# Expert stage of a two-layer block: one 128-column token tile, unsplit down weights, and a new order of work within an expert

## The reference, cut to what matters

```python
combine = jnp.sum(one_hot(expert_id, 32) * weight[..., None], axis=1)      # two experts for each token
hid = silu(einsum('td,edf->tef', tk, w1)) * einsum('td,edf->tef', tk, w3)  # 1024 -> 256, twice
hid = hid * c[:, :, None]
y   = einsum('tef,efd->td', hid, w2)                                       # 256 -> 1024
```

## Time and profile before

| what | value |
|---|---|
| median of 3 runs | 1771.48 us (1768.0 to 1773.71) |
| the profiled execution | 1772.76 us |
| its span, first to last instruction | 1770.7 us |
| TensorE busy | 1523.5 us, 86% |
| VectorE busy | 948.3 us, 54% |
| ScalarE busy | 714.9 us, 40% |
| mean granted TensorE clock | 0.925 of full speed |

### The profile page before, as it was taken

One profiled execution on the slowest core, in us unless ns is written; L12 is line 12 of the kernel. 1 busy time (PEld: TensorE's weight loads), 2 busy tenths in 40 slices (PEclk: granted clock), 3 DMA queues, 4 the chain that ended last, 5 costly groups with the idle time before them and its releaser, 6 DMA issues.

```text
span 1770.7 us, 17596 instructions
## 1 busy us (share of the span) xinstructions
PE 1523.5 (86%) x7159; PEld 1147.0 (65%) x7159; DVE 948.3 (54%) x1301; ACT 714.9 (40%) x1043; POOL 68.2 (4%) x80
## 2 busy tenths in 40 slices
PE   5999997798786963899999991989697899999999
PEld 4888775586565842555555551868585877678887
DVE  3444246623763445788888874675545535321334
ACT  4333334424443220666666662244322215652231
POOL 1000000000000000111011101000000000000000
PEclk9999998998997986899999996999897988999999
DMA  6422221122104430999999984220101003002241
GB/s 197 168 96 75 96 73 66 68 75 72 70 26 161 152 119 23 307 327 340 331 336 335 329 294 156 72 71 26 47 1 48 1 24 119 1 1 72 95 143 48
DMA packets 80348, 224.01 MB, mean 127 GB/s; under 512 B 9044, under 2 KB 10182, under 8 KB 76167
## 3 DMA queue, kind: packets, MB, share of 16 engines
q1 hardware_dynamic: 71558, 193.73, 32.3%
q0 software_dynamic: 6144, 20.71, 3.5%
q10 hardware_dynamic: 2560, 8.39, 1.3%
HBM read 200.00 MB, written 22.81 MB: 126 GB/s over the span
## 4 chain that ended last, share of the span: by engine, by line
PE 59%; DVE 25%; ACT 11%; DMA 2%; issue 2%; SPq 1%; POOL 0%; DVEq 0%; POOLq 0%; ACTq 0%
PE PS L502 14%; PE PS L504 14%; PE PS L503 14%; DVE wlo L1152 7%; DVE htlo L1152 5%; PE PS L928 4%; ACT whi L1950 3%; PE PS L499 3%; DVE ylo L1152 2%; ACT work L1950 2%; PE PS L1077 2%; ACT yhi L1950 2%; PE PS L1068 1%; ACT hthi L1950 1%; DVE work L1561 1%
## 5 line engine op out<-in xcount | busy, mean ns | idle before, releaser
L1152 DVE TENSOR_TENSOR wlo<-raw,whi 128x2048 fp32r<-128x2048 f32 x74 | 169.1, 2291 | 356.3 <-ACT whi L1950 356.3
L1950 ACT ACTIVATE whi<-raw 128x2048 fp32r<-128x2048 f32 x74 | 141.2, 1912 | 334.9 <-PE PS L504 333.5
L499 PE MATMUL PS<-consts,work 128*128 128x128 f32 (+1 forms) x652 | 100.7, 298 | 125.9 <-DVE work L1178 53.2
L502 PE MATMUL PS<-whi,hthi 128*128 128x512 f32 x480 | 200.1, 417 | 9.2 <-ACT work L1950 6.4
L502 PE MATMUL PS<-hthi,whi 128*128 128x512 f32 x480 | 198.3, 413 | 5.1 <-ACT scratch L1950 2.8
L503 PE MATMUL PS<-wlo,hthi 128*128 128x512 f32 x480 | 190.9, 398 | 0.0
L504 PE MATMUL PS<-whi,htlo 128*128 128x512 f32 x480 | 190.8, 398 | 0.0
L504 PE MATMUL PS<-hthi,wlo 128*128 128x512 f32 x480 | 190.0, 396 | 0.0
L503 PE MATMUL PS<-htlo,whi 128*128 128x512 f32 x480 | 189.5, 395 | 0.0
L499 PEld LDWEIGHTS PS<-consts,work 128*128 128x128 f32 (+1 forms) x652 | 85.2, 182 | 155.1 <-DVE work L1178 54.4
L1950 ACT ACTIVATE work<-PS 128x512 f32<-128x512 f32 (+3 forms) x204 | 103.3, 531 | 88.6 <-PE PS L992 51.2
(11 more groups left out here) (320 smaller groups left out, 2600.3 us busy)
## 6 DMA issues: line engine op xcount, KB each, us to landing
raw<-in_w_in SPq DMA_DIRECT2D x44, 1024.0 KB
raw<-in_w SPq DMA_DIRECT2D x80, 512.0 KB
scratch<-in_w SPq DMA_DIRECT2D x48, 512.0 KB
raw<-in_w SPq DMA_DIRECT2D x19, 1024.0 KB
scratch<-in_w SPq DMA_DIRECT2D x13, 1024.0 KB
raw<-in_w_gate SPq DMA_DIRECT2D x8, 1024.0 KB
raw<-in_w_out SPq DMA_DIRECT2D x8, 1024.0 KB
y_scratch<-work ACTq DMA_DIRECT2D x32, 256.0 KB, 7.1
```

The source lines that it names most:

```text
L499: return e.transpose(o, i, ident[0:n, 0:n])
L502: e.matmul(o, lh, rh, start=start, stop=False)
L1152: tt(lo, raw_place(j), as_f32(hi), SUB).then_inc(*ve.mark("lo", j))
L1950: return e.activation(o, i, f, bias=bias, scale=scale)
```

## The change

1. `bring` puts the high and the low part of a token tile side by side in one tile `G` of 128 columns. `up` multiplies that tile by the high and by the low half of the weights: 16 matmuls in place of 24. Partitions 0 to 63 of the result are the products of the high tokens, 64 to 127 those of the low tokens. ScalarE copies the lower half down (`low_half`) and VectorE adds (`join`) into `UPS`.
2. The down unit is not split. `down` multiplies the hidden tile, unsplit and padded with zeros to 128 columns (`HT`), by the raw unit in plain fp32: 4 matmuls in place of 12. A down unit now keeps its raw slot until `down` is done (`pe["unit", ...]`).
3. Slots in the stage: 7 raw (3 of `raw`, 2 in the second halves of `yhi`/`ylo`, 2 lent by `scratch`), 4 split. Two more units can be loaded and two more up units are split before the stage.
4. Order in step n: TensorE up(n), hand_over(n-1), bring(n+1), down(n-1). ScalarE split, hand_over(n-1), low_half(n), split, bring(n+1), gate_hidden(n), down(n-1). VectorE split, bring(n+1), join(n), low_tokens(n+1), hidden(n), split. The splits of step n are those of up(n+2).

```diff
-    LENT_RAW, LENT_SPLIT = 2, 3
+    LENT_RAW, LENT_SPLIT = 4, 2
...
+    G = yhi[:, 0:4, :].rearrange("p a n -> p (a n)").rearrange("p (u k n) -> p u k n", u=2, k=KD)
+    GHI, GLO = G[:, :, :, 0:CAP], G[:, :, :, CAP:2 * CAP]
+    HT = y_plain[:, 1, 0, :].rearrange("p (u k n) -> p u k n", u=2, k=2)
...
-                    m = passes(ps[0:CAP, :], GHI[:, u, kk, :], GLO[:, u, kk, :], wh[:, :, k, :], wl[:, :, k, :],
-                               kk == 0, kk == KD - 1)
+                    e.matmul(ps, G[:, u, kk, :], wh[:, :, k, :], start=kk == 0, stop=False)
+                    m = e.matmul(ps, G[:, u, kk, :], wl[:, :, k, :], start=False, stop=kk == KD - 1)
...
+                on.wait_ge(*raw_got[raw_slot[j]][j])
+                on.wait_ge(*ve["blank"])
+                on.wait_ge(*ac["out", "hidden", n])
                 for k in range(2):
-                    m = passes(PS[0:CAP, bank.of[key], :], HHI[:, u, k, :], HLO[:, u, k, :], wh[:, k, cols],
-                               wl[:, k, cols], k == 0, k == 1)
+                    m = e.matmul(ps, HT[:, u, k, :], w[:, k, cols], start=k == 0, stop=k == 1)
...
         for n in range(NE + 1):
+            if n < NE:
+                up(n)
+            if n:
+                hand_over(n - 1)
             if n + 1 < NE:
                 bring(n + 1)
-            if n:
-                hand_over(n - 1)
-            if n < NE:
-                up(n)
             if n:
                 down(n - 1)
...
+            elif raw_prior[j] in whole:
+                on.wait_ge(*pe["unit", raw_prior[j]])
             elif raw_prior[j] is not None:
                 on.wait_ge(*ve["lo", raw_prior[j]])
...
+        def join(n):
+            u = n % 2
+            on.wait_ge(*ac["low half", n])
+            tt(UPS[:, u, :], UPS[:, u, :], inside("up", n)[0:CAP, :], ADD).then_inc(*ve.mark("out", "up", n))
...
         for n in range(NE + 1):
+            if n + 2 < NE:
+                split()
+            if n:
+                hand_over(n - 1)
+            if n < NE:
+                low_half(n)
+            if n + 2 < NE:
+                split()
             if n + 1 < NE:
                 bring(n + 1)
```

More of the change, by code:

```diff
@@ L346, in build @@
     UNITS = len(units)
+    whole = {unit["down", n][0] for n in range(NE)}
+    to_split = [j for j in range(UNITS) if j not in whole]
     raw_slot, split_slot, raw_prior, split_prior = {}, {}, {}, {}
     raw_in, split_in = {}, {}
+    for q, j in enumerate(to_split):
+        q -= to_split.index(MOE) if j < TWO else to_split.index(TWO) - 1
+        split_slot[j] = q % NS if j < MOE or j >= TWO else q % (NS + LENT_SPLIT)
+        split_prior[j] = split_in.get(split_slot[j])
+        split_in[split_slot[j]] = j
     for j in range(UNITS):
@@ L783, in hand_over @@
             pv = ps[:, 0:2 * CAP].rearrange("p (k n) -> p k n", k=2)
-            on.wait_ge(*ve["out", "up", n])
+            on.wait_ge(*ve["hidden", n])
             for k in range(2):
@@ L807, in down @@
             u, j = n % 2, unit["down", n][0]
-            wh, wl = (a.rearrange("p (k n) -> p k n", k=2) for a in split_place(j))
+            w = raw_place(j).rearrange("p (k n) -> p k n", k=2)
             for half in range(2):
[L810 to L815, removed]
+                cols = slice(half * BANK, half * BANK + BANK)
+                ps = fresh("down", n, half)
+                on.wait_ge(*raw_got[raw_slot[j]][j])
+                on.wait_ge(*ve["blank"])
+                on.wait_ge(*ac["out", "hidden", n])
                 for k in range(2):
-                    m = passes(PS[0:CAP, bank.of[key], :], HHI[:, u, k, :], HLO[:, u, k, :], wh[:, k, cols],
-                               wl[:, k, cols], k == 0, k == 1)
-                m.then_inc(*pe.mark(*key))
-                bank.filled(key)
+                    m = e.matmul(ps, HT[:, u, k, :], w[:, k, cols], start=k == 0, stop=k == 1)
+                m.then_inc(*pe.mark("down", n, half))
+                bank.filled(("down", n, half))
             pe.also("unit", j)
@@ L1146, in split @@
         def split():
-            j = next_unit[0]
+            j = to_split[next_unit[0]]
             next_unit[0] += 1
@@ L2173, in scalar @@
             split()
-        normalise("n2", g2, lambda i: ve["out", "wo", 1, i])
+        normalise("n2", g2, lambda i: ve["out", "wo", 1, i], [split, split])
         on.wait_ge(*ve["ex"])
@@ L2212, in scalar @@
         bring(0)
-        for _ in range(LENT_SPLIT):
-            split()
         for n in range(NE + 1):
+            if n + 2 < NE:
+                split()
+            if n:
+                hand_over(n - 1)
+            if n < NE:
+                low_half(n)
+            if n + 2 < NE:
+                split()
             if n + 1 < NE:
                 bring(n + 1)
[L2218 to L2221, removed]
             if n < NE:
-                if next_unit[0] < TWO:
-                    split()
                 gate_hidden(n)
-                if next_unit[0] < TWO:
-                    split()
             if n:
                 down(n - 1)
+        split()
         ac.also("experts")
@@ L2584, in sync @@
         e.dma_start(xw, xv).then_inc(*xw_got.mark("all"))
-        for j in range(first_out + NR, MOE + NS + NR):
+        for j in range(first_out + NR, MOE + NS + NR + 2):
             load(j)
@@ L2590, in sync @@
         e.dma_start(xn_dram.rearrange("(i p) d -> p i d", p=P), xs).then_inc(*xn_put.mark("all"))
-        for j in range(MOE + NS + NR, TWO + NR + 1):
+        for j in range(MOE + NS + NR + 2, TWO + NR + 1):
             load(j)
```

80 lines of the change are left out of this document (42 added, 38 removed).

## The result

The changed kernel takes **1883.36 us** (median of 4 runs, 1880.01 to 1886.51) against 1770.28 us (1768.0 to 1773.71, 4 runs) for the kernel before: a ratio of 1.0631, 95% interval 1.0611 to 1.065. The forecast of 1820 us had the direction and the mechanism; the time lies 33 us above its range.

What follows compares the result with a forecast made beforehand. The prediction took a VectorE and ScalarE loop of 10.99 us an expert to bound the kernel before, DMA 0.3 us behind; 26 x (13.1 - 10.99) = 55, less 6, gives +49 on 1772.8: forecast 1820 us, range 1777 to 1850.

Steps and rivals of the forecast that it cites:

- the mechanism: Expert stage: down done, load of up(n+3) issued, unit landed, ScalarE's split, hand-over, next down; one new loop per expert.
- The work per engine: Expert stage, busy time per expert: VectorE about 7.5 us, ScalarE about 7.3, TensorE 8.9, against 10.99 us an expert before.
- the prediction's own sign of being wrong: Wrong if down's matmuls differ much from 0.95 us, scalings are 10.7 us apart with DMA at its limit, or ScalarE never idles.
- the sum of the loop's length: Expert stage: 5.1 + 0.8 + 1.9 + 0.3 + 3.8 + 0.2 = 12.1 us an expert, 13.1 with the clock's fall.
- down's end to the unit usable: Loop's load: 5.1 us, from a lone load's 4.6 plus wake, issue and notice, and 0.8 for the store sharing the engines.
- The clock: TensorE in the stage: granted clock about 0.8, its fall meeting down and adding 1.0 us an expert, bounds 0 and 2.
- The first four experts: Start of the stage: DMA engines get four units, then run dry; 42 us expected where it was 40.
- The tail: Stage's end after the last scaling: no splits or subtraction in the last two steps, so 26 us shrinks by some 9.
- The loop at full clock: Rival for the expert stage: the loop without the clock's fall, +23 us, 1795 us; chance 0.25.
- The longer loop: Rival for the expert stage: transfers slowed by 1.4 us or down wholly at 1.2 GHz, 14.5 us an expert, 1857 us; chance 0.12.
- The rival by which DMA sets the pace: Rival for the expert stage: the loop doesn't bind, DMA does at 10.7 us an expert, about -21, 1751 us; chance 0.12.
- The lone load of the prediction: A 1.05 MB load in the kernel before, issued at 590.41 with nothing beside it, taking 4.6 us to its last byte.

Runs made afterwards that it cites:

- edit 1: Changed kernel with the seven raw slots dealt out as four for up units and three for down units: 1740.99 us, 0.9787 of the kernel before.
- edit 2: Changed kernel with one raw slot fewer, six in place of seven: 1945.07 us, 1.0953 of the kernel before.
- edit 4: Changed kernel with four unneeded fp32 matmuls added before down's wait, to keep TensorE busy: 1844.84 us, 1.0389 of the kernel before.
- edit 5: Changed kernel with two of the four fp32 matmuls of down left out: 1800.68 us, 1.0128 of the kernel before.
- edit 6: Changed kernel storing 4 of each expert's 64 rows, the rest zeroed once near the start: 1876.07 us, 1.0565 of the kernel before.
- edit 7: Changed kernel with SyncE waiting for the unit held by down to land before issuing the next two: 1845.77 us, 1.0395 of the kernel before.
- edit 3: Changed kernel with ScalarE's hand-over put ahead of the first split in each step: 1811.4 us, 1.0207 of the kernel before.

## Why the prediction was right and wrong

**The mechanism was right.** The wait, the unit behind it, the split in front of the hand-over and the burst of three are in the chain as they were derived from the order of the code. That the loop goes through the slots is shown by edit 1 (removed, 15.00 to 9.64 us) and edit 2 (lengthened, 17.05 us); that down is a link of it by edits 4 and 5. The work per engine was right too, and so was the price of a plain fp32 matmul at full clock: 0.91 us a call, against 0.95 predicted. In the loop a call took 1.5 us in the mean (5.91/4), so the prediction's own sign of being wrong, matmuls of down that take much more than 0.95 us, came true.

**The step that failed is the sum of the loop's length**, 13.1 us for 15.0, in two terms of about the same size:

| term | predicted | measured |
|---|---|---|
| down's end to the unit usable | 5.1 + 0.8 | 6.9 |
| split, hand-over, semaphores | 1.9 + 0.3 + 0.2 | 2.2 |
| down | 3.8 + 1.0 | 5.9 |

The first is the mean landing of 6.50 us and 0.39 us before it on the chain, the last the mean of 24 turns.

1. *Landing, 1.0 us short.* I priced the load by a lone one and added only the store. The store is worth 0.23 us of landing and 0.36 us of distance (edit 6), not 0.8, so it is the 5.1 us that was too small, by some 1.6 us. From a burst's first issue to the landing of its first unit the engines move 1.41 million bytes in the mean: the 1.05 of the unit, 0.21 of the store and 0.15 of the units issued behind it. The last would be worth 0.4 us at 342 GB/s (an estimate). The prediction itself says that loads come in bursts of three, but its sum doesn't use it. The rest is a slow start that the lone load doesn't show, and its cause stays open (below).
2. *The clock, 1.1 us short.* The granted clock was forecast well (0.8 to 0.9, measured 0.80), and so was where it falls. Its price was not: down takes 5.9 us where it needs 3.65 at full clock, 2.3 us more and not 1.0; edit 4 gives 1.7 back as a lower bound, and in edit 7 down is 1.8 us shorter where up stands right before it. A pause of 4.2 us right before down puts most of down at 1.2 GHz, not an average share of it. The Trainium skill ("TensorE: Matmul & The Clock Gate", HAM oscillation) tells of a loop in which each group of matmuls after a wait for a DMA starts at the low clock and loses half of the time that it spends there; the trace agrees, with 0.50 granted at the start of down and 2.3 of 5.9 us lost.

The two feed each other, since a later landing makes a longer pause. With the 0.2 us by which the split and the hand-over were shorter, and times 26 experts, they make 49 of the 62 us by which the change in span exceeded the forecast.

**Start and end were off as well.** The first four experts lost 9.6 us and not 2: the DMA engines ran dry as predicted, but 8.2 of the 9.6 us are in the third and fourth distance (13.66 and 15.33 us, before 9.81 and 10.99), so the loop held from there on. The tail gave 2.7 us and not 9. Its chain has no split left, as forecast; but it meets three downs of 3.6 to 3.7 us, and its last store lands in 5.49 us where the last one took 2.85, which the prediction left out. Behind the stage the rest of the kernel is 6 us longer. This does not hang on the loop: counted from the last scaling to the end it is 726 us before, 730 in the change and 734 in edit 1. From 100 to 500 us after the last scaling the granted clock is 0.91 and 0.86 in place of 0.93 and 0.88, which at 173 and 184 us of TensorE's busy time would be some 8 us at most (an estimate), but why it is lower was not tried.

**The rivals.** The loop at full clock (12.1 us, 1795 us) is what edit 4 should have been, had landing been right; it gave 13.28. The longer loop (14.5 us, 1857 us) was nearest: its condition, transfers slowed by 1.4 us *or* down wholly at 1.2 GHz, should have been an "and" with smaller sizes. I gave it 0.12, arguing that idler DMA engines would not slow a transfer; they are idle on average, but in the burst, where the transfer is, their share is 0.85 and more from the second microsecond on. The rival by which DMA sets the pace is what the change does once the slots don't couple, but at 9.64 us and not 10.7. The DMA share of 0.97 read as "at its limit" was wrong: at a share of 1.01 the same engines move 375 GB/s, 13% more. The Trainium skill ("Perfetto Trace Analysis", Identifying the Most-Contended Engine) calls occupancy misleading for the 16 DMA engines and wants bytes used instead; the trace agrees, 0.97 at 332 GB/s and 1.01 at 375.

**What stays open.** The first packets of a burst are slow in the change: 4096-byte packets take 258 to 336 ns in the mean of the first 5 us after the second issue, burst by burst, and 159 ns two microseconds later. Single microseconds of the burst at 891.86 show it:

```profile
892.00:893.00 1.00, 1.00 (x6) 0.82 (x5) 0.47 (x1) 0.09 (x1) 0.00 (x0) 1.00 0.40 78
893.00:894.00 1.00, 1.00 (x6) 0.83 (x5) 0.00 (x0) 0.00 (x0) 0.00 (x0) 1.00 1.15 295
894.00:895.00 1.00, 1.00 (x5) 0.59 (x4) 0.00 (x0) 0.00 (x0) 0.00 (x0) 1.00 0.85 143
895.00:896.00 1.00, 1.00 (x9) 0.94 (x9) 0.00 (x0) 0.00 (x0) 0.00 (x0) 1.00 0.91 242
...
897.00:898.00 1.00, 0.00 (x0) 0.00 (x0) 0.00 (x0) 0.00 (x0) 0.55 (x1) 0.71 0.97 352
898.00:899.00 1.00, 0.00 (x0) 0.00 (x0) 0.00 (x0) 0.66 (x1) 0.00 (x0) 0.50 1.02 418
```

The lone load of the prediction reached 412 GB/s from 2.6 to 3.6 us after its issue, where this burst has 143 to 242. The store and the next units account for more bytes, but not for 143 GB/s at a share of 0.85. Without the store the landing is 6.27 us (edit 6), and the second units of edit 7, with one unit behind them in place of two and no store beside them, take 5.62. These two readings fit a price for what is issued behind, but they differ in more than that, and no run has a burst with nothing else under way. The cause was not separated.

## What to carry to other kernels

When a buffer is to be released by a later consumer, count which load in the queue gets that slot, what stands behind that load, and which instruction of which engine needs it: here seven slots dealt out by kind rather than in rotation turn 6.3% slower into some 2.2% faster, with the same work and memory. Price a link of such a loop under the conditions of the loop: a load in the burst that it comes in, and a matmul after the pause that the loop itself makes. An edit that removes one wait of an engine with a fixed order puts another instruction in front, so follow the order of all engines around once more (edit 3) before it is taken for a cure. And when an experiment gives the number that was expected, look whether the term that it was made for has moved: in edit 7 the distance came out to 0.02 us, and the landing hardly moved.

## What the runs showed of the hardware

- The DMA engines' busy share says little about what is left: 0.97 at 332 GB/s in the kernel before, 1.01 at 375 to 379 GB/s for nearly the same transfers.
- The first of three units issued in a burst (1.05 million bytes, two transfers) lands 6.50 us after its second issue in the mean (6.21 to 7.38). Without the store beside it, it is 6.27 (edit 6); with a unit ahead of it and none behind it 6.24 (edit 7, first units); with one unit behind it and none ahead 5.62 (edit 7, second units).
- A plain fp32 matmul of 512 columns with 128 columns of weights takes 0.91 us at full clock; four after a pause of 4.2 us take 5.1 to 6.7 us in place of 3.65. Four matmuls of no use ahead of them kept the clock at 1.00 and made the kernel 39 us faster.
